# A first stage on transposed tokens, and a rewritten order of work where the expert stages begin and end

## What is computed

```python
# first block
mod = silu(c) @ ada_w + ada_b                  # 6 x 1024
sh1, sc1, g1, sh2, sc2, g2 = split(mod, 6)
h = rmsnorm(x, norm1_g) * (1 + sc1) + sh1
x = x + g1 * hybrid_mixer(h)                   # projection w_in, SSD and gated delta rule, w_out
h = rmsnorm(x, norm2_g) * (1 + sc2) + sh2
x = x + g2 * moe_ffn(h)                        # router: top 4 of 32 experts
x = rmsnorm(x, final_g)
# second block
x = x + hybrid_mixer_2(rmsnorm(x, g_mix))      # sparse attention and gated linear attention
x = x + hier_moe(rmsnorm(x, g_ffn))            # top group of 4, then top 2 of its 8 experts
return rmsnorm(x, g_final)
```

## Time and profile before

| | us |
|---|---|
| median of 3 runs | 2229.33 |
| lowest, highest | 2229.11, 2230.70 |
| the profiled execution, its own time | 2227.41 |
| its span in the trace | 2225.7 |
| PE busy in the span | 2078.5 |
| HBM bytes read | 706.85 MB |

### The profile page before, as it was taken

One profiled execution on the slowest core, in us unless ns is written; L12 is line 12 of the kernel. 1 busy time (PEld: TensorE's weight loads), 2 busy tenths in 40 slices (PEclk: granted clock), 3 DMA queues, 4 the chain that ended last, 5 costly groups with the idle time before them and its releaser, 6 DMA issues. The chain is left out here.

```text
span 2225.7 us, 25010 instructions
## 1 busy us (share of the span) xinstructions
PE 2078.5 (93%) x10093; PEld 1056.0 (47%) x10093; DVE 547.9 (25%) x1154; ACT 368.4 (17%) x626; POOL 97.7 (4%) x171
## 2 busy tenths in 40 slices
PE   3999999989999999999999999799899899999998
PEld 1768676654444433333334333355464444444443
DVE  1436543442222211221122212322342200000001
ACT  2133431210000000000000000213341111111112
POOL 0101042010000000000000000100030000000000
PEclk7999999989999999999999999899999899999999
DMA  9233163559999999999999999834253499999995
GB/s 334 95 123 114 38 240 115 209 204 427 428 428 429 428 428 429 428 428 428 429 429 428 429 428 429 309 114 164 60 189 150 180 428 429 429 428 428 429 429 243
DMA packets 98749, 708.59 MB, mean 318 GB/s; under 512 B 12306, under 2 KB 17900, under 8 KB 61580
## 3 DMA queue, kind: packets, MB, share of 16 engines
q1 hardware_dynamic: 98700, 707.92, 77.3%
HBM read 706.85 MB, written 1.05 MB: 318 GB/s over the span
## 5 line engine op out<-in xcount | busy, mean ns | idle before, releaser
L1584 PE MATMUL ps<-ring,arena 128*64 128x512 f32 x2048 | 452.0, 594 | 28.5 <-DMA ring<-in_moe_w_gu 28.5
L1584 PEld LDWEIGHTS ps<-ring,arena 128*64 128x64 f32 x2048 | 161.2, 137 | 312.9 <-issue 247.3
L1606 PE MATMUL ps<-ring,arena 128*64 128x512 f32 x1024 | 226.8, 594 | 19.6 <-issue 19.6
L2750 PE MATMUL ps<-ring,arena 128*64 128x512 f32 x1024 | 224.7, 593 | 6.7 <-DMA ring<-in_w_up 5.3
L1606 PEld LDWEIGHTS ps<-ring,arena 128*64 128x64 f32 x1024 | 84.6, 137 | 141.2 <-issue 141.2
L2750 PEld LDWEIGHTS ps<-ring,arena 128*64 128x64 f32 x1024 | 77.9, 137 | 150.3 <-issue 150.3
L1637 ACT ACTIVATE arena<-arena 128x512 f32<-128x512 f32 x32 | 20.1, 630 | 767.9 <-DVE arena L1683 767.9
L2021 PE MATMUL ps<-ring 128*128 128x512 f32 (+1 forms) x320 | 139.9, 587 | 1.4 <-DVE ring L2483 0.8
L2771 PE MATMUL ps<-ring,arena 128*64 128x512 f32 x512 | 113.4, 595 | 0.0
L1683 DVE TENSOR_SCALAR arena<-ps 128x512 f32<-128x512 f32 x32 | 22.1, 691 | 332.3 <-PE ps L1584 332.3
L2811 DVE TENSOR_SCALAR arena<-iota_row,arena 128x64 f32<-128x64 f32 x68 | 12.6, 249 | 326.8 <-PE ps L2750 325.3
(11 more groups left out here) (561 smaller groups left out, 2064.8 us busy)
## 6 DMA issues: line engine op xcount, KB each, us to landing
ring<-in_moe_w_gu SPq DMA_DIRECT2D x128, 2048.0 KB, 24.1
ring<-in_moe_w_down SPq DMA_DIRECT2D x64, 2048.0 KB, 21.4
ring<-in_w_down SPq DMA_DIRECT2D x32, 2048.0 KB, 12.1
ring<-in_w_gate SPq DMA_DIRECT2D x32, 2048.0 KB, 14.8
ring<-in_w_up SPq DMA_DIRECT2D x32, 2048.0 KB, 17.2
ring<-in_w_in SPq DMA_DIRECT2D x22, 2048.0 KB, 11.5
ring<-in_ada_w SPq DMA_DIRECT2D x12, 2048.0 KB, 10.2
ring<-in_w_out SPq DMA_DIRECT2D x6, 2048.0 KB, 8.4
```

Of the source, the lines that this page charges most:

```text
L1584: last = M.matmul(ps[halves[j], 4 + which, :], xgT[buf][:, k, CAP * ee:CAP * ee + CAP], w[:, k2, at:at + 512], start=False, stop=(k == KD ...
L1606: last = M.matmul(ps[halves[j], 6, :], yT[:, k % KH, halves[k // KH]], w[:, k % KH, 512 * j:512 * j + 512], start=(k == 0), stop=(k == 2 * ...
L2750: last = M.matmul(ps[halves[j], 4 + which, :], xgT[:, k, halves[j]], w[j][:, k, :], start=(k == 0), stop=(k == KD - 1))
```

## The change

**First stage.** It is joined to the block of the projection. SP loads three small sets of rows first (`c`, `ada_b`, `norm1_g`, as 32 rows of 128), then the first `ada_w` chunk, `x`, three more chunks in the order 0, 2, 1, 3 (half of shift, half of scale, and the other halves), the convolution rows, three chunks of `w_in`, and only then the small parameters. The normed tokens are transposed before shift and scale are applied. Four products with one column of ones give shift and scale as columns; DVE applies them while it takes the transposed tokens out of PSUM, one feature chunk (128 features by 256 tokens) in each operation, half of the features after the second chunk and half after the fourth. The first unit of the projection waits for each feature chunk by itself. Its banks are shifted by four.

**First router and expert stage 1.** Logits are formed with the router's weights as stationary operand, in four groups of 32 partitions (`partial_logits`), taken by ACT (`lgp`), and folded by one product per tile. The residual is put into PSUM earlier. The one-hot matrix, the first gather, the zeroed buffers and the first bias selector move into the router's block. The tables for the bias choice (`pick`, `quarter`, `fold2`) are made once by POOL in the first stage. The down bias is added in every turn by two products from rows of `b_down` (L1666 of the changed kernel); the four products after the loop are gone, and so are the transposes of the gates. The bias selector has two buffers.

**Second block.** The compression rows are loaded at the start of expert stage 1. The first unit of the projection waits for the first tile only. The router gets `partial_logits` in two groups of 64 partitions with zero-padded weights (POOL clears them), the norm is split in two DVE operations, ACT squares both tiles before it takes the first transposed one, the choice of group takes four operations instead of eight, and one-hot matrix and first gather move ahead as in the first block.

```diff
-            for j in range(4):
-                modulation_sums(pe, cond, 4 + j % 2)
-                pe.wait_ge(s_part, j + 1)
-                M.matmul(ps[:, j, :], ones[:, :], mod_part).then_inc(s_comb, 1)
...
-            vv(V.tensor_tensor(modB, banks(0, 2, 1024), abias[:, 0:D], ALU.add))
-            vv(V.tensor_tensor(modA, banks(2, 2, 1024), abias[:, D:2 * D], ALU.add))
-            vv(V.scalar_tensor_tensor(modA, modA, 1.0, n1g, ALU.add, ALU.mult))
-            for t in range(T):
-                vv(V.tensor_tensor(hn[:, t, :], hn[:, t, :], modA, ALU.mult))
-                V.tensor_tensor(hn[:, t, :], hn[:, t, :], modB, ALU.add).then_inc(s_h, 1)
...
+            sp.dma_start(rowsC[24:32, :], a["norm1_g"][0].rearrange("(c p) -> c p", p=P)).then_inc(s_rowc, 16)
+            ra.load(sp, 1)
+            sp.dma_start(x_res, a["x"][0].rearrange("(t p) d -> p t d", p=P)).then_inc(s_x, 16)
+            ra.load(sp, 4)
...
+            sp.dma_start(rowsB[48:60, :], a["ssd_conv_b"][0].rearrange("(c p) -> c p", p=P)).then_inc(s_rows, 16)
+            ra.load(sp, 7)
...
+            def early_sums(i):
+                modulation_sums(pe, cond, 4 + i % 2)
+                pe.wait_ge(s_part, i + 1)
+                if i == 2:
+                    pe.wait_ge(s_cw, 3)
+                for q in range(4):
+                    last = M.matmul(ps[:, 7 - i // 2, 4 * (i % 2) + q:4 * (i % 2) + q + 1],
+                                    early_parts[i % 2][:, q * P:(q + 1) * P], ones[:, 0:1])
+                last.then_inc(s_comb, 1)
+            pe.wait_ge(s_const, 1)
+            pe.wait_ge(s_rowc, 48)
+            M.transpose(ps[:, 7, 0:32], rowsC[0:32, :], ident[0:32, 0:32]).then_inc(s_first, 1)
+            pe.wait_ge(s_cw, 1)
+            early_sums(0)
+            for t in range(T):
+                pe.wait_ge(s_h, t + 1)
+                for k in range(KD):
+                    last = M.transpose(ps[:, k // 2, (k % 2) * 256 + t * P:(k % 2) * 256 + (t + 1) * P],
+                                       hn[:, t, k * P:(k + 1) * P], ident[:, :])
+            last.then_inc(s_first, 1)
+            early_sums(1)
+            pe.wait_ge(s_rows, 48)
+            M.transpose(ps[:, 6, 0:96], rowsA[0:96, :], ident[0:96, 0:96])
+            M.transpose(ps[:, 6, 96:156], rowsB[0:60, :], ident[0:60, 0:60]).then_inc(s_first, 1)
+            early_sums(2)
+            early_sums(3)
...
+            bias = acol[:, 8:24].rearrange("p (m k) -> p m k", m=2)
+            for half in range(2):
+                dve.wait_ge(s_cw, 1)
+                dve.wait_ge(s_comb, 2 * half + 2)
+                mc, at = shift_scale[:, half, :, :], slice(4 * half, 4 * half + 4)
+                vv(V.tensor_tensor(mc, ps[:, 7 - half, 0:8].rearrange("p (m k) -> p m k", m=2), bias[:, :, at], ALU.add))
+                vv(V.scalar_tensor_tensor(mc[:, 1, :], mc[:, 1, :], 1.0, acol[:, 24 + 4 * half:28 + 4 * half], ALU.add, ALU.mult))
+                dve.wait_ge(s_first, 2)
+                for q in range(4):
+                    k = 4 * half + q
+                    V.tensor_scalar(hT[:, k, :], ps[:, k // 2, (k % 2) * 256:(k % 2) * 256 + 256], mc[:, 1, q:q + 1], mc[:, 0, q:q + 1],
+                                    ALU.mult, ALU.add).then_inc(s_hk, 1)
+            dve.wait_ge(s_cw, 3)
...
+            def partial_logits(t):
+                for r in range(2):
+                    pe.wait_ge(s_h2Tt, 2 * t + r + 1)
+                    for g in range(4):
+                        last = M.matmul(ps[32 * g:32 * g + 32, 4 + 2 * t, 0:P], rw[:, 4 * r + g, :], h2T[:, 4 * r + g, toks(t)],
+                                        start=(r == 0), stop=(r == 1))
+                last.then_inc(s_lp, 1)
             def router_logits(t):
-                pe.wait_ge(s_res, 3 + t)
-                for k in range(KD):
-                    if k % 4 == 0:
-                        pe.wait_ge(s_h2Tt, 2 * t + k // 4 + 1)
-                    last = M.matmul(ps[:, 4 + t, 0:NE], h2T[:, k, toks(t)], rw[:, k, :], start=(k == 0), stop=(k == KD - 1))
-                last.then_inc(s_lg, 1)
+                pe.wait_ge(s_lpt, t + 1)
+                M.matmul(ps[:, 5 + 2 * t, 0:NE], lgp[:, t, :], pick[:, 0:NE]).then_inc(s_lg, 1)
             normed_transposes(0)
+            start_from_residual(0)
             pe.wait_ge(s_n2, 48)
+            pe.wait_ge(s_res, 4)
+            partial_logits(0)
+            start_from_residual(1)
+            normed_transposes(1)
             router_logits(0)
-            normed_transposes(1)
+            partial_logits(1)
+            router_logits(1)
             pe.wait_ge(s_nm, 1)
             first_ranks(4)
-            router_logits(1)
-            start_from_residual(0)
             pe.wait_ge(s_nm, 2)
             second_ranks(4).then_inc(s_rk, 1)
-            start_from_residual(1)
+            pe.wait_ge(s_one1, 1)
+            for half in range(2):
+                gather_half(h2, onehot1, half, 6 + half, s_xg1)
...
+            first_slots(dve, 4, s_rk, s_slot1)
+            dve.wait_ge(s_iota, 1)
+            make_onehot(onehot1, first_slot_of, 0, s_one1)
...
+            pass_count(4)
+            V.memset(y21, 0.0).then_inc(s_y21, 1)
+            V.memset(GT1, 0.0).then_inc(s_GTt1, 1)
+            V.tensor_scalar(bsel1[0], bcast(quarter, CAP), pick[:, 0:1], None, ALU.mult).then_inc(s_bs1, 1)
...
+                for j in range(2):
+                    sp.dma_start(bias_dn[32 * j:32 * j + 32, :], a["moe_b_down"][0][:, 512 * j:512 * j + 512]).then_inc(s_bdn, 16)
+                for i, kv in enumerate("kv"):
+                    sp.dma_start(pos_rows[16 * i:16 * i + 16, :], a[f"cmp_pos_{kv}_2"][0].rearrange("(j i) d -> j (i d)", i=2)).then_inc(s_p9, 16)
+                    sp.dma_start(pos_rows[32 + 2 * i:34 + 2 * i, :], a[f"cmp_b1_{kv}_2"][0].rearrange("(k p) -> k p", p=P)).then_inc(s_p9, 16)
...
+                            for j in range(2):
+                                M.matmul(ps[halves[j], 6, :], bsel[ee][:, j, :], bias_dn, start=True, stop=False)
...
-                pe.wait_ge(s_g2, 1)
-                for t in range(T):
-                    for d in range(2):
-                        M.matmul(ps[:, 2 * t + d, :], gT[0:NE, t * P:(t + 1) * P], bdn[0:NE, 512 * d:512 * d + 512],
-                                 start=False, stop=False, skip_group_check=True)
...
-            pe.wait_ge(s_uTt, 4)
+            pe.wait_ge(s_uTd, 2)
             for u in range(FIRST):
                 j, t = divmod(u, 2)
+                if u == 1:
+                    pe.wait_ge(s_uTt, 2)
                 if t == 0:
...
+            def partial_logits(t):
+                for r in range(4):
+                    if r % 2 == 0:
+                        pe.wait_ge(s_nTt, 2 * t + r // 2 + 1)
+                    for j in range(2):
+                        last = M.matmul(ps[halves[j], 4 + 2 * t, 0:P], rw2[:, 2 * r + j, :], h2bT[:, 2 * r + j, t * P:(t + 1) * P],
+                                        start=(r == 0), stop=(r == 3))
...
+            start_from_residual(0)
             pe.wait_ge(s_p11, 80)
+            partial_logits(0)
+            pe.wait_ge(s_r11, 2)
+            start_from_residual(1)
+            transpose_normed(1)
             router_logits(0)
-            transpose_normed(1)
+            partial_logits(1)
             router_logits(1)
-            start_from_residual(0)
             pe.wait_ge(s_m11, 1)
-            first_ranks(6)
-            start_from_residual(1)
+            first_ranks(4)
             pe.wait_ge(s_m11, 2)
-            second_ranks(6).then_inc(s_k11, 1)
+            second_ranks(4).then_inc(s_k11, 1)
+            pe.wait_ge(s_one2, 1)
+            for half in range(2):
+                gather_half(h2b, onehot2, half, 6 + half, s_xg2)
...
+                vv(V.tensor_tensor(xg3, x_res[:, t, :], fgn, ALU.mult))
                 dve.wait_ge(s_rt11, t + 1)
                 vv(V.reciprocal(ss3[:, t:t + 1], ss3[:, t:t + 1]))
-                V.scalar_tensor_tensor(by_stripe(h2b[:, t, :]), x_res[:, t, :].rearrange("p (q k) -> p q k", k=KD), ss3[:, t:t + 1],
-                                       fgn.rearrange("p (q k) -> p q k", k=KD), ALU.mult, ALU.mult).then_inc(s_n11, 1)
+                V.tensor_scalar(by_stripe(h2b[:, t, :]), xg3.rearrange("p (q k) -> p q k", k=KD), ss3[:, t:t + 1],
+                                None, ALU.mult).then_inc(s_n11, 1)
...
-                select_top(dve, lg8[:, t, :], 1, gm8[:, t, :], gsel[:, t, :], tmpe[:, 0:8], s1)
+                select_first(lg8[:, t, :], gm8[:, t, :], gsel[:, t, :], tmpe[:, 0:8])
```

386 lines of the change are left out of this document (184 added, 202 removed).

## The result

The changed kernel takes 2192.36 us (median of 4 runs, 2191.13 to 2193.63) against 2229.22 us (2227.81 to 2230.70) for the kernel before, a ratio of 0.9835 with a 95% interval of 0.9818 to 0.9852: 36.9 us or 1.7% faster. The forecast was 2194.4 us, with a range of 2186 to 2208. The profiled execution has a span of 2189.4 us, 36.3 shorter than before.

The account below looks back on a forecast made before the run. Expert stages were taken as bound by DMA bytes, with PE, ACT and DVE chains between. Gains 18.1 + 4.2 + 8.2 + 4.4 = 34.9 us off 2227.4 give 2192.5 profiled, 2194.4 as median; range 2186 to 2208.

Parts of the forecast that it names:

- The bound: Both expert stages: DMA streams at 428 GB/s set the time; whatever brings their first products forward is kept to the end.
- rival 4: Whole kernel: gains don't reach the end because the streams are bound by bytes, about 2210 us; chance 0.03.
- First stage: Kernel start: reordered loads and a shorter chain bring DVE's first convolution unit from 62.3 to 44.2 us, gain 18.1 us.
- The bounds of 39.1 and 47.6: First convolution unit: 39.1 us with fast sums and one-column products (gain 23), 47.6 with slow sums and first unit (14.7).
- First router: First router to first expert: earlier routing and a 5.36 us gather start the expert's products at 490.3 us, gain 4.2.
- Expert stage 1: Two products added per turn fit PE's waits, costing 0.3 us once in the last turn; 2.6 us saved at the scatter.
- Rival 3: Expert loop becomes the bound once a turn grows by over 0.9 us; 2.5 us added gives 2244 us; chance 0.03.
- The seam: Second block's start: compression rows long there and unit 0 bound to the first tile alone, 5.6 us saved.
- the loop's end: After the first expert loop: four products of 3.69 us go, the scatter still waits for DVE; 2.6 us saved.
- Second router: Second router to first pair's products: earlier, shorter routings of 4.0 us and a gather of 5.36, gain 4.4 us.
- Rival 1: Half clock at both gathers, the first biases and the projection's first unit: 2204 us, chance 0.15; sign: gathers over 6 us.
- The rule against the change: Before both gathers: residual's 512-wide products restore full clock, so taking them away leaves both gathers cold from first to last.

## Why the prediction was right, step by step

The time came out 2.0 us under the forecast, and every part within 1.4 us of its sum. The mechanism, a stream that is started earlier by four shortened chains, was shown by the runs; that the total lies so close is in part luck, of which the paragraphs below give the pieces.

**The bound.** The forecast rested on reading an expert stage as a stream that is started, not shortened: what brings its first products forward is kept. That held. Expert stage 1 took 925.5 to 926.7 us in ten profiles whose first products started anywhere from 465.2 to 488.3 us, and the kernel with the first stage alone carried its 13 us to the end (rival 4, at 2210, is out).

**First stage, 18.1 forecast, 19.5 in the profile.** Landings were forecast to 0.2 us: first chunk 10.2 against 10.1, rows 29.5 against 29.7. The chain behind them was given 14.7 us and took 13.1. Two terms were too dear: four one-column products at 1.5 us (from the weight load of L1253) took 1.05, and the last set of sums at 3.09 took 1.92, the clock being full again. One was too cheap: from DVE's last feature chunk to the first convolution it is 1.27 us, not the 0.45 of a last product. The kernel before has a spread here too: its first stage, unaltered, began the convolution at 60.29 us in the kernel with all but the first stage, and against that the gain is 17.5. Over the eight profiles whose first stage is that of the change, and no edit touches it, the first convolution lies between 42.5 and 49.3, mean 44.1; forecast 44.2. The bounds of 39.1 and 47.6 were too narrow on the late side: 47.73 and 49.26 lie outside. The bound let the clock hurt the sums and the first unit. In the slowest profile, 1.7 us later than the bound, 0.5 are one-column products (1.8 a set at half clock, 1.5 in the sum) and 0.8 the stretch from the joined projection's start to the convolution (6.8 us for 6.0).

**First router, 4.2 against 4.4.** The gather at 5.36 was 5.21, and other executions had 5.25 to 5.46, 6.62 and 6.67. The block boundary was given 0.65 us and took 1.83: the register load for the number of passes had run beside the gather when both stood in one block, and the forecast overlooked that moving the gather uncovers it. The ranks took 1.15 us for 0.6. Against that the second tile's transposes took 1.04 us for 1.85, taken from a row at half clock, and the one-hots 0.8 for 1.47, so that the sum hides these misses: here the number is luck. No run undoes one router alone; their gains are read between marks of the profiles, which give 4.2 us for each router in the kernel with all but the first stage.

**Expert stage 1, 2.6 against 2.3.** The reasoning that the pair fits into 0.6 us of issue and 0.9 of ring is what the runs show. Rival 3's condition was read right in kind, and the price is now known: 0.82 us a pair, free up to 0.79 us a turn. With three pairs more the kernel is slower than the one before (ratio 1.0093, 1.0072 to 1.0113), which is this rival come true.

**The seam, 5.6 against 5.8; together with the loop's end 8.2, as forecast.** Undoing the rows alone costs 6.5, of which 1.7 are that PE waits longer for them than it did in the kernel before; the first unit's earlier start is worth 1.0.

**Second router, 4.4 against 4.2.** A routing takes 3.9 us (forecast 4.0), the first one starts at 1692.2 on the new time scale, 7.6 us after the transposes; 8.1 were forecast. The ranks took 1.16 us for 0.55 and the gather 5.62 for 5.36, so that these misses cancel as well.

**What the forecast did not have.** It priced the clock only where it changes code. In 404 us before the router and 277 in the second block it moved the profile by -2.4 and +4.1, in places where the change alters single instructions at most. The two nearly cancel with the -1.6 of stage 2, so the balance came out 1.4 us from the forecast partly by luck. Rival 1, both gathers cold throughout, didn't come: three profiles drew 6.6 to 6.7 at the first gather, over the 6 us that the forecast had named as the sign of this rival, but none had the 7.4 of a gather at half clock throughout. A gather at full clock takes 3.84 us, so what the rival names cost 1.4 to 2.8 us a gather in the profiles.

**The rule against the change.** The prediction read from the earlier trace rows that the clock was full again after the residual's 128x512 products. That is so at the first router, where it rises to 0.83 at 484 to 486 us among these products. At the second it does not carry to the gather: the same products stand at 1730 to 1737 us, the clock is at 1.00 and 0.98 from 1734 to 1741, PE stands still for 4.04 us, and from 1741 the clock is 0.50. So the rows did not bear the rule out at the second router. What the runs show is that with products in PE's waits at the routers both gathers take 3.73 to 3.84 us.

## What to carry to other kernels

In a kernel with a stream that is bound by its bytes, add up what stands ahead of the stream's first release and count it one for one; count work inside the stream only from the point at which PE's waits for the ring are used up, and price it by a second run with more of it rather than by its busy time. When work moves across a block boundary, look at what it was covering: here a register load of 0.86 us came out from behind a gather. And before explaining a few microseconds between two profiles, compare the granted clock of the stretch: identical code differed by 4 us there, so that one profile of each kernel can't tell an effect of this size from the draw.

## What the runs showed of the hardware

- Filling TensorE's waits with products that nobody reads keeps the clock up for what stands behind them: transposes 1.97 us for 3.68, a gather 3.84 for 5.21 to 6.67, a unit of the projection 3.69 for 6.26. The time gains only where that work is next on the path. In short waits it depends on the place: at the first router, in waits of 1.4 us, the clock fell all the same (0.50) and the fillers overran by up to 0.9 us; at the second router the same fillers ran at full clock.
- A register load between two rows of products costs next to nothing on the array: no gap at the first gather, 0.23 us at the second. Alone at the head of a block it costs 0.86 us (1.83 less 0.97). The change from one block to the next costs another 0.97 us before the first expert.
- The executions of the changed kernel spread over 6.4 us (5 of them). With the fillers in all places the mean clock is higher, 0.991 to 0.994 for 0.984 to 0.987, but the spread is no smaller (6.0 us).
